# Gate and up products of a two-block transformer kernel: high and low token halves joined into one 512-column operand, a bank each, modulation sums spread

## What is computed

```python
gate, up = jnp.split(h @ w_gate_up, 2, axis=-1)
return (jax.nn.silu(gate) * up) @ w_down
```

## Time and profile before

| | |
|---|---|
| runs | 1138.37 us median of 3 (1136.17 to 1141.06) |
| the profiled execution | 1137.21 us, of which 1135.4 us are the span from first to last instruction |
| TensorE matmul busy | 1036.1 us, 91% |
| VectorE busy | 683.4 us, 60% |
| ScalarE busy | 444.3 us, 39% |
| mean granted TensorE clock | 0.961 of full |

### The profile page before, as it was taken

The page is one execution under the profiler, slowest core; times in us unless marked ns, Lnnn a source line. Parts: engine busy times, 40 slices in busy tenths (PEclk is TensorE's granted clock), DMA queues, the critical chain, the costliest instruction groups (busy, mean ns, idle before and its releaser), DMA issues.

```text
span 1135.4 us, 16076 instructions
## 1 busy us (share of the span) xinstructions
PE 1036.1 (91%) x6560; PEld 924.7 (81%) x6560; DVE 683.4 (60%) x1264; ACT 444.3 (39%) x683; POOL 48.1 (4%) x70
## 2 busy tenths in 40 slices
PE   6999869999999899977999999789979859999996
PEld 5877659999988888756999988687756649999985
DVE  2656566777755755456777764756764545555543
ACT  3445324333333355424333333354444344333331
POOL 5100010000000200001000000100000000000000
PEclk8999998999999999898999999989987989999998
DMA  8643029988754554115998865453410026666550
GB/s 268 219 144 111 1 74 270 286 261 259 279 172 133 171 176 142 45 38 172 277 279 252 279 225 164 148 176 123 132 54 1 1 74 171 181 180 181 184 181 38
DMA packets 191274, 185.09 MB, mean 163 GB/s; under 512 B 7082, under 2 KB 160837, under 8 KB 191200
## 3 DMA queue, kind: packets, MB, share of 16 engines
q1 hardware_dynamic: 188288, 175.85, 50.4%
q0 software_dynamic: 2768, 7.87, 2.4%
q10 hardware_dynamic: 144, 0.33, 0.1%
HBM read 182.97 MB, written 1.06 MB: 162 GB/s over the span
## 4 chain that ended last, share of the span: by engine, by line
PE 79%; DVE 12%; ACT 5%; issue 2%; POOL 1%; DMA 1%; SPq 0%; POOLq 0%; DVEq 0%; ACTq 0%
PE ps L960 14%; PE ps L1001 11%; PE ps L1002 11%; PE ps L1003 11%; PE ps L1317 5%; PE ps L938 5%; PE ps L940 4%; PE ps L939 4%; PE ps L1045 3%; DVE wl L1666 3%; PE ps L1055 2%; ACT wh L1436 1%; DVE probs L1883 1%; ACT probs L1460 1%; PE ps L1080 1%
## 5 line engine op out<-in xcount | busy, mean ns | idle before, releaser
L1666 DVE TENSOR_TENSOR wl<-raw,wh 128x2048 fp32r<-128x2048 f32 (+5 forms) x147 | 319.6, 2176 | 219.2 <-ACT wh L1436 219.0
L1436 ACT ACTIVATE wh<-raw 128x2048 fp32r<-128x2048 f32 (+5 forms) x147 | 268.2, 1824 | 443.1 <-PE ps L1003 247.1
L1001 PE MATMUL ps<-xh,wh 128*128 128x256 f32 x1056 | 302.9, 287 | 3.3 <-DVE xl L1684 2.0
L1002 PE MATMUL ps<-xl,wh 128*128 128x256 f32 x1056 | 301.8, 286 | 0.0
L1003 PE MATMUL ps<-xh,wl 128*128 128x256 f32 x1056 | 301.6, 286 | 0.0
L1001 PEld LDWEIGHTS ps<-xh,wh 128*128 128x128 f32 x1056 | 204.6, 194 | 4.4 <-issue 4.4
L1002 PEld LDWEIGHTS ps<-xl,wh 128*128 128x128 f32 x1056 | 204.7, 194 | 0.0
L1003 PEld LDWEIGHTS ps<-xh,wl 128*128 128x128 f32 x1056 | 204.5, 194 | 0.0
L938 PE MATMUL ps<-wh,xh 128*128 128x384 f32 (+5 forms) x288 | 108.2, 376 | 16.4 <-DVE xl L1678 6.4
L940 PE MATMUL ps<-wh,xl 128*128 128x384 f32 (+5 forms) x288 | 102.1, 354 | 0.0
L939 PE MATMUL ps<-wl,xh 128*128 128x384 f32 (+5 forms) x288 | 102.0, 354 | 0.0
(11 more groups left out here) (254 smaller groups left out, 1191.1 us busy)
## 6 DMA issues: line engine op xcount, KB each, us to landing
raw<-in_w_down SPq DMA_DIRECT2D x33, 1024.0 KB, 5.0
adaw<-in_w_ada SPq DMA_DIRECT2D x24, 1024.0 KB, 7.1
raw<-in_w_gate SPq DMA_DIRECT2D x44, 512.0 KB, 4.4
raw<-in_w_up SPq DMA_DIRECT2D x44, 512.0 KB, 5.8
raw<-in_w_gate_up SPq DMA_DIRECT2D x44, 512.0 KB, 5.2
raw<-in_w_in SPq DMA_DIRECT2D x12, 768.0 KB, 4.5
raw<-in_w_in SPq DMA_DIRECT2D x8, 1024.0 KB, 5.1
raw<-in_w_o SPq DMA_DIRECT2D x8, 1024.0 KB, 5.0
```

The source lines that it names most:

```text
L1001: mm(o, a[:, v, k, :], xh[:, k, :], start=k == 0, stop=False)
L1002: mm(o, a[:, v, k, :], xl[:, k, :], start=False, stop=False)
L1436: me.go(activation(wh[:, m % NW, 0:n], raw[:, ITEM[item] % NRAW, 0:n], ACT.Copy), wh_ready)
L1666: me.go(V.tensor_tensor(wl[:, m % NW, 0:n], raw[:, ITEM[item] % NRAW, 0:n], wh[:, m % NW, 0:n].bitcast(F32), ALU.subtract), wl_ready)
```

## The change

On TensorE each step (v, k) becomes two matmuls in place of three. `xh` and `xl` become the two halves of one tile `xhl`, and the weight's high part multiplies both in one matmul of 512 columns: high tokens go to columns 0 to 255 of a bank, low tokens to 256 to 511. The weight's low part multiplies the high tokens into columns 0 to 255. So gate and up take a bank each (4 and 5 in even items, 6 and 7 in odd ones), and each holds two sums that still have to be added.

That is done behind. ScalarE copies the low-token half out of PSUM (`crossed`), VectorE adds the other half to it; this is done for gate and for up. ScalarE then takes the silu from SBUF in place, VectorE multiplies, ScalarE (no longer VectorE) writes `gh`, and VectorE writes `gl`. The order within an item changes as well: both engines now do the steps of item i first and the split of item i + 3 after them, with `gh` and `gl` behind the split.

The modulation's operations are spread by a table: in items 1 to 21 one each, two in every third item, then 4, 4, 4, 3, 3, 2 in the first six items of the down product. There are 48 as before. The twelve loads and the six `ada(q)` follow: `ada` after gate-and-up items 8, 14 and 19 (bank 0), and after items 2, 4 and 7 of the down product (banks 5, 6, 7); VectorE copies the first three in items 10, 16 and 21.

```diff
-ADA_LOAD = {2 * m + 4: m for m in range(12)}
-ADA_GU = {4 * n + 6: n for n in range(4)}
-ADA_DN = {1: 4, 5: 5}
+ADA_OPS = [0] + [1 + (i % 3 == 0) for i in range(1, 22)] + [4, 4, 4, 3, 3, 2]
+ADA_AT = [i for i, n in enumerate(ADA_OPS) for _ in range(n)]
+ADA_LOAD = {ADA_AT[4 * m - 5] + 6 if m > 1 else 2 * m + 4: m for m in range(12)}
+ADA_GU = {8: 0, 14: 1, 19: 2}
+ADA_DN = {2: 3, 4: 4, 7: 5}
...
-            put(("gu", L, i), 4 + i % 4, "dve")
+            for v in range(2):
+                put(("gu", L, i, v), 4 + 2 * (i % 2) + v, "dve")
...
-            put(("ada", ADA_Q[L][4]), 6, "dve")
-            put(("ada", ADA_Q[L][5]), 7, "dve")
+            for n in range(3):
+                put(("ada", ADA_Q[L][3 + n]), 5 + n, "dve")
...
-        xh = sb("xh", [P, KC, S], F32R)
-        xl = sb("xl", [P, KC, S], F32R)
+        xhl = sb("xhl", [P, 2, KC, S], F32R)
+        xh, xl = xhl[:, 0], xhl[:, 1]
...
-                    bank = claim(("gu", L, i))
                     for v in range(2):
-                        o = ps[:, bank, v * S:(v + 1) * S]
+                        bank = claim(("gu", L, i, v))
                         for k in range(KC):
...
-                            mm(o, a[:, v, k, :], xh[:, k, :], start=k == 0, stop=False)
-                            mm(o, a[:, v, k, :], xl[:, k, :], start=False, stop=False)
-                            ins = mm(o, b[:, v, k, :], xh[:, k, :], start=False, stop=k == KC - 1)
-                    fill(ins, ("gu", L, i))
+                            if k == KC - 1:
+                                mm(ps[:, bank, 0:S], b[:, v, k, :], xh[:, k, :], start=False, stop=False)
+                            ins = mm(ps[:, bank, :].rearrange("p (c n) -> p c n", c=2), a[:, v, k, :], xhl[:, :, k, :], start=k == 0, stop=k == KC - 1)
+                            if k < KC - 1:
+                                mm(ps[:, bank, 0:S], b[:, v, k, :], xh[:, k, :], start=False, stop=False)
+                        fill(ins, ("gu", L, i, v))
...
+            def crossed(L, i, v):
+
+                key = ("gu", L, i, v)
+                wait_full(act, key)
+                me.go(activation((gsilu, gated)[v][:, i % 4, :], ps[:, U.bank[key], S:2 * S], ACT.Copy), cross_ready)
+
             def gates(L):
                 for i in range(NGU):
+                    crossed(L, i, 0)
+                    wait_done(act, ("gu", L, i, 0))
+                    me.go(activation(gsilu[:, i % 4, :], gsilu[:, i % 4, :], ACT.Silu), silu_ready)
+                    crossed(L, i, 1)
                     feed(split, ("gu", L, i), ("gu", "dn"))
-                    key = ("gu", L, i)
-                    wait_full(act, key)
-                    me.go(activation(gsilu[:, i % 4, :], ps[:, U.bank[key], 0:S], ACT.Silu), silu_ready)
+                    act.wait_ge(product_ready, NGU * L + i + 1)
+                    me.go(activation(gh[:, i, :], gated[:, i % 4, :], ACT.Copy), upper_ready)
...
             def ffn(L):
                 for i in range(NGU):
+                    for v, o in enumerate((gsilu[:, i % 4, :], gated[:, i % 4, :])):
+                        key = ("gu", L, i, v)
+                        dve.wait_ge(cross_ready, 2 * (NGU * L + i) + v + 1)
+                        me.empty(V.tensor_tensor(o, ps[:, U.bank[key], 0:S], o, ALU.add), key)
+                    me.settle()
+                    dve.wait_ge(silu_ready, NGU * L + i + 1)
+                    me.go(V.tensor_tensor(gated[:, i % 4, :], gsilu[:, i % 4, :], gated[:, i % 4, :], ALU.mult), product_ready)
+                    if L < 2:
+                        modulations(L, i)
                     feed(split, ("gu", L, i), ("gu", "dn"))
...
+                    dve.wait_ge(upper_ready, NGU * L + i + 1)
+                    me.go(V.tensor_tensor(gl[:, i, :], gated[:, i % 4, :], gh[:, i, :].bitcast(F32), ALU.subtract), gated_ready)
                     if L < 2 and i - 2 in ADA_GU:
                         ada(ADA_Q[L][ADA_GU[i - 2]])
```

More of the change, by code:

```diff
@@ L575, in released @@
     if k == "gu":
-        return ("full", item)
+        return ("full", (*item, 1))
     if k == "wo" and item[2] == KC // 2 - 1:
@@ L731, in program @@
         landed = [sem(f"landed{i}") for i in range(NRAW)]
-        wh_ready, wl_ready, cols_ready, silu_ready, gated_ready = (
-            sem(n) for n in ("wh_ready", "wl_ready", "cols_ready", "silu_ready", "gated_ready"))
+        wh_ready, wl_ready, cols_ready, silu_ready, cross_ready, product_ready, upper_ready, gated_ready = (
+            sem(n) for n in ("wh_ready", "wl_ready", "cols_ready", "silu_ready", "cross_ready", "product_ready", "upper_ready", "gated_ready"))
         s_cst, s_const, s_vec, s_bias_out, s_bias_in, s_out = (sem(n) for n in ("s_cst", "s_const", "s_vec", "s_bias_out", "s_bias_in", "s_out"))
@@ L1713, in _, with modulations @@
             partial = [None]
+            def modulations(L, at_item):
+                for o in range(len(ADA_AT)):
+                    if ADA_AT[o] == at_item:
+                        modulation(L, o // 2, o % 2)
             def modulation(L, u, n):
@@ L1735, in ffn @@
                 for i in range(NGU):
-                    feed(split, ("gu", L, i), ("gu", "dn"))
[L1737 to L1750, removed]
+                    for v, o in enumerate((gsilu[:, i % 4, :], gated[:, i % 4, :])):
[7 more added lines that the diff above has]
+                        modulations(L, i)
+                    feed(split, ("gu", L, i), ("gu", "dn"))
+                    dve.wait_ge(upper_ready, NGU * L + i + 1)
+                    me.go(V.tensor_tensor(gl[:, i, :], gated[:, i % 4, :], gh[:, i, :].bitcast(F32), ALU.subtract), gated_ready)
                     if L < 2 and i - 2 in ADA_GU:
@@ L1754, in ffn @@
                     feed(split, ("dn", L, i), "dn")
[L1755 to L1759, removed]
+                    if L < 2:
+                        modulations(L, NGU + i)
+                    if L < 2 and i in (3, 5):
+                        ada(ADA_Q[L][3 + (i == 5)])
                 if L < 2:
```

## The result

| | before | changed |
|---|---|---|
| median | 1138.12 us (1136.15 to 1141.06, 9 runs) | 1143.08 us (1141.9 to 1147.59, 9 runs) |
| ratio to before | | 1.005, 95% interval 1.0037 to 1.0063 |
| span of the profiled execution | 1135.4 us | 1141.3 us |

The changed kernel is 5 us slower. First the page of the changed kernel: busy time of the engines, the lines of the chain that ended last, and, from the list of waits, TensorE's wait before the down product.

What follows compares the result with a forecast made beforehand. The prediction took TensorE's matmul spacing as the bound, plus its wait before the down product. Its terms -11.3 + 9.2 + 4.8 = +2.7 us on the profiled 1137.2 made 1139.9, plus 1.2 to the median: 1141.1 us, range 1132 to 1149.

Steps and rivals of the forecast that it cites:

- The matmuls: Gate and up stage: a step falls from 359.1 to 348.1 ns, over 1056 steps, -11.3 us after 0.3 off for half clock.
- the price of the joined matmul: Gate and up stage: a 512-column matmul costs 228.4 ns, taken from the down product's dense matmuls; bounds 213.3 and 239.4.
- Its own sign of being wrong: Gate and up stage: joined matmuls spaced other than 228 ns would show the prediction wrong.
- The Trainium skill's 2.5 ns: Gate and up matmuls: by this alternative figure all steps save 2.6 us in place of 11.3, giving 1149.8 us.
- The start of the down product: Layers 0 and 1: TensorE waits 5.6 us for VectorE's copy in place of 1.0, +9.2 us in all.
- T: End of the last gate and up matmul's slot, 304.74 us in the kernel before; the wait was counted from it.
- The clock: Behind the down product's wait, layers 0 and 1: clock falls to half, 2.4 us each, +4.8 us; chance it stays up 0.10.
- The engines behind: Gate and up stage: VectorE and ScalarE loops of 5.52 and 5.94 us an item keep up with TensorE, costed at nothing.
- 5.71 us: Gate and up stage: mean loop per item from which ScalarE and VectorE become the bound, giving 1147 us; chance 0.17.
- the first term: Gate and up matmuls in all three layers: joining them saves 11.3 us.

Runs made afterwards that it cites:

- e4: e1 with the high and low half of a chunk side by side, one contiguous 2 KB operand in place of two pieces 8 KB apart: 1129.01 us.
- e1: The changed kernel with VectorE's copy of an ada sum to modv one item after its matmuls in place of two: 1127.94 us, ratio 0.9902.
- e7: The kernel before with the fourth ada after item 19 in place of 18, so VectorE's copy stands at the end of item 21: 1153.15 us, ratio 1.0124.
- e3: The changed kernel with 22 more matmuls of 512 columns on TensorE in the wait before the down product, layers 0 and 1: 1145.27 us.
- e5: e1 with modulation operations as dense as in the kernel before, two in every item from 1 on: 1125.08 us, ratio 0.9874.
- e2: The kernel before with VectorE's copy one item after its ada matmuls, the same edit as e1: 1146.01 us, ratio 1.0055.

## Why the prediction was nearly right

Forecast were 1141.1 us, 1132 to 1149, with no difference (within 0.5%) as the likeliest class and slower as the second. Measured are 1143.08 us, 5 us or 0.5% slower, right at the edge between the two, and 2.0 us above the forecast.

- **The matmuls, -11.3 forecast, -8.2 measured.** The step that failed is the price of the joined matmul, "228.4, the one row with that width". That row is a stream of one width. Taking turns with 256 columns, a step costs 352.5 ns and not 348.1, which is 4.6 us over 1056 steps; grouped by width it costs 349.2. Its own sign of being wrong, joined matmuls spaced other than 228 ns, did show. In return the old step was 360.0 ns and not 359.1, about 1 us more saved, and an `ada` call lengthened the old stage by 0.89 us and the new one by 0.82, which gives some 0.6 beyond the moved calls. Layout was not to blame, as e4 shows. The Trainium skill's 2.5 ns over the columns of a warm matmul (TensorE: Matmul & The Clock Gate, "Wait — 56ns, not 53.3ns?") was not borne out: by it a step saves 2.5 ns, and it saved 7.5 (360.0 to 352.5), or 10.8 with the widths grouped.
- **The start of the down product, +9.2 forecast, +9.2 measured.** 5.60 us was worked out from rows and 5.61 measured, and the steps fit one by one: the addition was put 0.60 us behind T, the product 1.05, the split 2.84, `gl` 5.05 and the copy 5.39, and they stand at 0.61, 1.07, 2.86, 5.06 and 5.40 behind 302.90. That is the mechanism, and not only the number. e1 takes the wait away and e7 makes it in the old kernel, at 6.48 where 6.5 was worked out.
- **The clock, +4.8 forecast, +4.2 measured.** It fell in both layers. e3 puts the price at 2.0 us in each by keeping TensorE busy in the same wait. The price is not the same behind every such wait: the half clock lasts 4.2 us of down matmuls here, and 3.0 us at a price of 1.4 in e7.
- **The engines behind, 0 forecast, 0 measured.** The loops of VectorE's items, in the timeline of the changed kernel:

```profile
198.26 0.41 DVE L1758 TENSOR_TENSOR scratch<-ps,scratch 128x256 f32<-128x256 f32 x1
...
204.33 0.42 DVE L1758 TENSOR_TENSOR scratch<-ps,scratch 128x256 f32<-128x256 f32 x1
...
209.86 0.42 DVE L1758 TENSOR_TENSOR scratch<-ps,scratch 128x256 f32<-128x256 f32 x1
...
215.38 0.41 DVE L1758 TENSOR_TENSOR scratch<-ps,scratch 128x256 f32<-128x256 f32 x1
```

  6.07 us with two modulation operations, 5.96 in e5 (5.94 worked out), and 5.52 with one (5.52 worked out). TensorE never waited for a bank or for `wl` inside the stage. Whether 5.71 us was the right point of decision is not shown. e5 ran at 5.92 without loss, but with more `ada` calls TensorE's own item is 5.84 there, and the copy stands an item earlier, so that a late VectorE does not lengthen that wait.

The terms sum to +2.7 forecast and +5.2 measured; the first term is 3.1 us off and the clock 0.6 the other way. The 0.7 us left in the spans lie outside all three.

Two things were luck. The forecast put 1.2 us between the profiled execution and the median, and the changed kernel's profiled execution is its median; that hid 1.2 of the 3.2 us by which the spans differ more than forecast. And the prediction, which says nothing of the mixers, needs them unchanged: layer 2's took 212.6 and 212.7 us in these two kernels, and up to 11.7 us more in others whose instructions there are the same.

## What to carry to other kernels

When a bank changes hands, look for the instruction that empties it in its engine's written order, and add up what stands ahead of it there: moved by one item that instruction cost 14 to 15 us (e1, e7), more than the 8 us that the optimization around it gained. An idle time of TensorE of that length is to be priced with the half clock behind it, 1.4 to 2.1 us here. And where the clock of an untouched stretch differs from version to version, judge an edit by the rows of its own part, and the whole by several versions.

## What the runs showed of the hardware

- Layer 2's mixer, with the same instructions in every version (some 950 matmuls) and with VectorE and ScalarE busy for the same time (124.5 to 125.0 and 93.7 us), took 212.6 to 224.3 us in twelve profiled executions, in step with its time at half clock (41 to 79 us). TensorE was far from idle in it: in e2 it stood at half clock for 41 us on end with matmuls in flight for 38. The time moves with the version (e2's six runs lay at 1142.1 to 1146.6, e5's four at 1123.3 to 1126.2) and with the execution (e3's seven at 1141.1 to 1149.4, clock 0.957 to 0.942).
- A stream in which float32r matmuls of 512 and 256 columns take turns takes 352.5 ns a pair, the same matmuls grouped by width 349.2; three matmuls of 256 columns, each with weights of its own, took 360.0.
- A moving operand in two pieces 8 KB apart is as quick as one of 2 KB: 2.82 and 2.81 us for eight pairs.
- A wait of 5.6 us of TensorE had the clock at half for 4.2 us of matmuls behind it and cost 2.1 us more than its own length (e1 against the changed kernel); one of 6.5 us had 3.0 us and cost 1.4 (e7); one of 1.0 us had none (kernel before).
